# Split-precision feed-forward products with the high weights times both token halves in one matmul, and normed tokens from the fifth pair on in the second feed-forward

## The reference, cut to what matters

```python
D_MODEL = 1024; SEQ = 256; D_FF = 2816

def rmsnorm(x, g):
    return x * rsqrt(mean(x * x, axis=-1) + EPS) * g
def modulate(h, shift, scale):
    return h * (1 + scale) + shift
def swiglu(h, w_in, w_out):
    gate, up = split(h @ w_in, 2, axis=-1)
    return (silu(gate) * up) @ w_out

# first feed-forward, tokens and context tokens
x   = x   + 0.5 * m[2]  * swiglu(modulate(rmsnorm(x, norm_ffn1), m[0], m[1]), w_ffn1_in, w_ffn1_out)
ctx = ctx + 0.5 * mc[2] * swiglu(modulate(rmsnorm(ctx, norm_ffn1), mc[0], mc[1]), w_ffn1_in, w_ffn1_out)
...   # mixer: x = x + m[5] * (mix @ w_mix_out)
# second feed-forward, tokens alone
x = x + 0.5 * m[8] * swiglu(modulate(rmsnorm(x, norm_ffn2), m[6], m[7]), w_ffn2_in, w_ffn2_out)
x = rmsnorm(x, final_norm)
...   # second block
```

## Time and profile before

| | |
|---|---|
| median of 3 runs | 1560.81 us (1559.29 to 1561.89) |
| span of the profiled execution | 1558.5 us |
| the profiled execution against the median | 2.3 us shorter, which includes what lies around the span |
| PE busy | 1417.4 us, 91% |
| DVE busy | 1083.1 us, 69% |
| ACT busy | 597.4 us, 38% |
| POOL busy | 381.5 us, 24% |
| output slices of f1, second round, split halves, on PE | 367.5 to 408.0 us |
| pairs of f2 on PE (258 columns) | 537.5 to 667.1 us |
| output slices of f2 on PE | 667.1 to 730.4 us |

### The profile page before, as it was taken

The page is one execution under the profiler, slowest core; times in us unless marked ns, Lnnn a source line. Parts: engine busy times, 40 slices in busy tenths (PEclk is TensorE's granted clock), DMA queues, the critical chain, the costliest instruction groups (busy, mean ns, idle before and its releaser), DMA issues.

```text
span 1558.5 us, 19836 instructions
## 1 busy us (share of the span) xinstructions
PE 1417.4 (91%) x7349; PEld 1053.8 (68%) x7349; DVE 1083.1 (69%) x2262; ACT 597.4 (38%) x1347; POOL 381.5 (24%) x376
## 2 busy tenths in 40 slices
PE   7899999999999999999999989999987777777777
PEld 5688888889888999999899955665433333233222
DVE  5976775557875687777897476766797666666554
ACT  5222222213556454444566143424343333333222
POOL 0000110001200100001007044545555444444330
PEclk9999999999999999999999999999999999999999
DMA  9754585545642366555545699999999999999997
GB/s 355 265 181 150 169 288 185 164 137 171 213 145 73 108 191 188 172 176 176 161 145 155 242 371 419 422 421 421 421 421 422 421 421 422 421 422 421 422 421 292
DMA packets 86191, 435.96 MB, mean 280 GB/s; under 512 B 9488, under 2 KB 13584, under 8 KB 53072
## 3 DMA queue, kind: packets, MB, share of 16 engines
q0 software_dynamic: 45024, 298.08, 47.6%
q1 hardware_dynamic: 41072, 136.62, 26.9%
HBM read 433.61 MB, written 1.05 MB: 279 GB/s over the span
## 4 chain that ended last, share of the span: by engine, by line
PE 60%; DMA 21%; DVE 13%; ACT 3%; issue 1%; POOL 0%; SPq 0%; ACTq 0%; DVEq 0%; POOLq 0%
PE ps L627 14%; PE ps L628 14%; PE ps L629 14%; DMA ring<-in_puv,AB 13%; PE ps L1059 10%; DMA HF<-in_puv,AB 7%; PE ps L979 5%; DVE WR L1455 2%; DVE ring L2255 1%; DMA ring<-in_w_ada 1%; ACT WR L1079 1%; PE ps L665 1%; DVE HF L2255 1%; DVE AB L1466 1%; PE ps L998 0%
## 5 line engine op out<-in xcount | busy, mean ns | idle before, releaser
L627 PE MATMUL ps<-HR,WR 128*128 128x512 f32 (+2 forms) x1064 | 344.5, 324 | 7.8 <-DVE WR L1455 6.7
L628 PE MATMUL ps<-HR,WR 128*128 128x512 f32 (+2 forms) x1064 | 340.3, 320 | 0.0
L629 PE MATMUL ps<-HR,WR 128*128 128x512 f32 (+2 forms) x1064 | 340.0, 320 | 0.0
L1455 DVE TENSOR_TENSOR WR<-ring,WR 128x1024 fp32r<-128x1024 f32 (+1 forms) x217 | 253.0, 1173 | 113.9 <-ACT WR L1079 113.8
L1079 ACT CAST WR<-ring 128x1024 fp32r<-128x1024 f32 (+1 forms) x217 | 212.5, 986 | 282.8 <-PE ps L629 282.6
L627 PEld LDWEIGHTS ps<-HR,WR 128*128 128x128 f32 x1064 | 203.3, 191 | 25.0 <-issue 7.2
L628 PEld LDWEIGHTS ps<-HR,WR 128*128 128x128 f32 x1064 | 203.4, 191 | 13.9 <-issue 0.2
L629 PEld LDWEIGHTS ps<-HR,WR 128*128 128x128 f32 x1064 | 203.2, 191 | 13.9
L1059 PE MATMUL ps<-AF,AB 128*128 128x512 f32 x264 | 128.3, 610 | 31.5 <-ACT AB L1440 31.5
L1430 ACT ACTIVATE AB<-AB 128x2 f32<-128x2 f32 x129 | 26.2, 203 | 324.6 <-DVE AB L2255 324.6
L627 PE MATMUL ps<-AR,WR 128*128 128x256 f32 (+1 forms) x471 | 147.8, 314 | 2.4 <-DVE AF L1848 2.4
(11 more groups left out here) (339 smaller groups left out, 2345.7 us busy)
## 6 DMA issues: line engine op xcount, KB each, us to landing
AB<-in_w_adaT POOLq DMA_DIRECT2D x56, 512.0 KB, 4.7
ring<-in_f1i SPq DMA_DIRECT2D x44, 512.0 KB, 4.7
ring<-in_f2i SPq DMA_DIRECT2D x44, 512.0 KB, 3.6
ring<-in_w SPq DMA_DIRECT2D x29, 512.0 KB, 3.7
ring<-in_f1o SPq DMA_DIRECT2D x21, 512.0 KB, 3.9
ring<-in_f2o SPq DMA_DIRECT2D x16, 512.0 KB, 4.1
ring<-in_w_ada SPq DMA_DIRECT2D x12, 512.0 KB, 9.4
ring<-in_mi SPq DMA_DIRECT2D x12, 512.0 KB, 4.3
```

Source lines behind the costliest of these rows:

```text
L627: e.matmul(o, l[0], r[0], start=first, stop=False)
L628: e.matmul(o, l[0], r[1], start=False, stop=False)
L629: return e.matmul(o, l[1], r[0], start=False, stop=last)
L1455: e.tensor_tensor(WS[:, m % NSP, 1, 0:nk * cols], ring[:, ring_of(m) % NS, 0:nk * cols], WS[:, m % NSP, 0, 0:nk * cols].bitcast(F32), ALU. ...
```

## The change

`two` stands beside `three`: one matmul with the high weights and a moving operand of high and low tokens side by side (2 x 256 columns), whose results go to the two halves of a PSUM bank, and one with the low weights and the high tokens, 256 columns, added to the first half. `project_apart` walks over the tiles with it. It is used for every product with 256 output columns in the two feed-forwards: the split halves of f1's last round, the eight output slices of f2, and the gates and ups of f2 from pair 4 on (RAWS = 4; the fifth pair). For those pairs the tokens are normed and modulated (in Hs, 256 columns without shift columns): POOL multiplies x by the gain and then by the norm factor (`ft`), ACT adds the shift and rounds, DVE makes the low part; ACT and DVE do this for k = 0 to 2 behind pair 1 and for k = 3 to 7 behind pair 2. The unnormed tokens of pairs 0 to 3 move to AR. Since a result now lies in two halves, they must be added: for pairs 4 to 21 ACT copies the second half of each result to SBUF and DVE adds the first; for output slices DVE makes two additions into XT instead of one, the second waiting for the first.

```diff
+RAWS = 4
+SCALED = {1: range(0, 3), 2: range(3, 8)}
...
-        raw = [Hs[:, n, :, 0:258] for n in range(2)]
+        raw = [AR[:, o:o + 2064].rearrange("p (k c) -> p k c", k=8) for o in (8960, 6656)]
+        ft = AB[:, 0:2048].rearrange("p (k t) -> p k t", k=8)
...
+            def two(o, l, r, first, last):
+                n = r[0].shape[1]
+                apart = o[:, 0:2 * n].rearrange("p (h t) -> p h t", h=2)
+                if first:
+                    e.matmul(apart, l[0], r[2], start=True, stop=False)
+                x = e.matmul(o[:, 0:n], l[1], r[0], start=False, stop=False)
+                return x if first else e.matmul(apart, l[0], r[2], start=False, stop=last)
...
+                            elif j >= RAWS:
+                                project_apart((st_, w, j), H256w, lambda k: dv.at("f2", "h", k))
...
+                        if z - a == 256:
+                            project_apart((st_, "out", rn, d, a), [(Ar[:, 0, k, a:z], Ar[:, 1, k, a:z], Ar[:, :, k, a:z])
+                                                                   for k in range(len(js))], lambda k: dv.at(st_, "act", js[k]))
```

On ACT:

```diff
+                            if j >= RAWS:
+                                q.wait_ge(*dv.at("f2", "act", j - 4))
+                                for w, dst in (("gate", raw_gate(j)), ("up", raw_up(j))):
+                                    q.wait_ge(*mm.at(st_, w, j))
+                                    e.copy(dst, bank_of(st_, w, j)[:, 256:512]).then_inc(*ac.to("low part", w, j))
...
+                            for k in SCALED.get(j, ()):
+                                q.wait_ge(*po.at("f2", "f", k))
+                                e.activation(H256[k][0], ft[:, k, :], ACT.Identity, bias=M[:, 48 + k, 0:1]).then_inc(
+                                    *ac.to("f2", "hi", k))
```

On DVE:

```diff
+                            if j >= RAWS:
+                                q.wait_ge(*ac.at("low part", "gate", j))
+                                e.tensor_tensor(g_, g_, og[:, 0:256], ALU.add).then_inc(*dv.to("ps", st_, "gate", j))
+                                dv.also("shift", "gate", j)
+                                q.wait_ge(*ac.at("low part", "up", j))
+                                e.tensor_tensor(u_, u_, ou[:, 0:256], ALU.add).then_inc(*dv.to("ps", st_, "up", j))
+                                q.wait_ge(*dv.now())
+                                q.wait_ge(*ac.at("silu", j))
+                                e.tensor_tensor(g_, u_, g_, ALU.mult).then_inc(*dv.to("gated", j))
...
+                            for k in SCALED.get(j, ()):
+                                q.wait_ge(*ac.at("f2", "hi", k))
+                                e.scalar_tensor_tensor(out=H256[k][1], in0=ft[:, k, :], scalar=M[:, 48 + k, 0:1],
+                                                       in1=H256[k][0].bitcast(F32), op0=ALU.add, op1=ALU.subtract).then_inc(
+                                                           *dv.to("f2", "h", k))
...
+                            if z - a == 256:
+                                e.scalar_tensor_tensor(out=XT[:, d, o], in0=src[:, 256:512], scalar=m2h[:, d, s:s + 1],
+                                                       in1=XT[:, d, o], op0=ALU.mult, op1=ALU.add).then_inc(
+                                                           *dv.to("low part", st_, d, a))
+                                q.wait_ge(*dv.now())
+                                src = src[:, 0:256]
```

On POOL, behind the sums of squares of the mixer's output ("mo"):

```diff
+            for k in range(8):
+                q.wait_ge(*dv.at("mo", "x", k))
+                e.tensor_scalar(ft[:, k, :], XT[:, k, 0:256], co[:, k, 0:1], None, ALU.mult).then_inc(*po.to("f2", "c", k))
+            for k in range(8):
+                q.wait_ge(*ac.at("root", "mo"))
+                q.wait_ge(*po.at("f2", "c", k))
+                e.tensor_tensor(ft[:, k, :], ft[:, k, :], R(2, 3), ALU.mult).then_inc(*po.to("f2", "f", k))
```

More of the change, by code:

```diff
@@ L388, in program @@
         H512 = [Hp(k, 0, 512) for k in range(8)]
+        H256w = [(*Hp(k, 0, 256), Hs[:, :, k, 0:256]) for k in range(8)]
         qN = AA[:, 0:1024].rearrange("p (i c) -> p i c", i=2)
@@ L1608, in ffn @@
                             og, ou = bank_of(st_, "gate", j), bank_of(st_, "up", j)
+                            if j >= RAWS:
[8 more added lines that the diff above has]
+                                q.wait_ge(*dv.now())
+                                parts((Ar[:, 0, i, :], Ar[:, 1, i, :]), g_, st_, "act", j)
+                                continue
                             q.wait_ge(*mm.at(st_, "gate", j))
```

32 lines of the change are left out of this document (26 added, 6 removed).

## The result

The changed kernel takes 1564.43 us (median of 14 runs, 1560.14 to 1566.28), the kernel before 1560.69 us in the same series (14 runs). The ratio is 1.0019, 95% interval 1.0012 to 1.0026: some 3 us slower (3.7 between the two medians), where 1.1 us faster was forecast. The profiled execution has a span of 1563.1 us, before 1558.5.

The account below looks back on a forecast made before the run. PE's pace was taken to bound mid-f2, DVE's chain the end of f1, DVE nearly full at f2's start. -4.75 - 2.34 + 3.0 + 2.9 + 0.1 = -1.1 us gave 1559.7 us; 8-in-10 range 1554.5 to 1565.0, own range 1557.7 to 1563.9.

Parts of the forecast that it names:

- End of f1: End of f1: DVE's second addition per split half makes q 1 start 3.0 us later, not 1.46 us earlier; bounds 1.5 to 4.0.
- hangs on q 1 and moves with it: Behind q 1: context norm's sum, reciprocal, root and scaling shift by the same 3.0 us as q 1.
- PE's pace: Wide plus narrow matmul replace three narrow ones per block: saves 4.75 us in f2's pairs, 2.34 in its slices.
- 0.2267 + 0.1200 = 0.3467: Cost in us of one block: a wide matmul at the pace of f1's 512-column ones plus a narrow 256-column one.
- The price of two pieces: Other bound for the wide matmul: a moving operand in two pieces costs two narrow matmuls, 0.2399 us.
- Start of f2: First pairs of f2: token low parts (3.2 us) and POOL's hold on DVE (2.0) stall PE 2.9 us; bounds 0.9 and 4.8.
- a single stall: Sign expected in the next profile: PE stalls only once at f2's start, in tiles 7 to 9.
- The 2.3 us by which the low parts were counted early: Start of f2: tile 9's low part, ready at 562.9 us, counted 2.3 us ahead of PE's need, as slack.
- End of f2: Behind f2's last slice: the second addition delays DVE's squares 0.52 us, mostly hidden; 0.1 us taken, at most 0.5.
- collide in full: Rival at f2's start: all sixteen POOL instructions cost DVE 0.48 us each, stall 8.6 us, 1565.4 us; chance 0.13.
- the wide matmul is not two narrow ones: Rival on PE's pace: wide matmul streams as two narrow ones, saving 0.9 us in all, 1565.9 us; chance 0.07.
- what POOL cost was not covered: Rival: POOL works in DVE's waits, f2 stalls 0.5 to 0.9 us, f1 loses 1.5 to 2; 1556.2 us, chance 0.29.

Follow-up runs that it names:

- experiment 6: Kernel before, with the new form (two matmuls a block, two additions) only in the five token halves of f1's last round: 1561.65 us, ratio 1.0007.
- experiment 7: Kernel before, with the new form only in the five context halves of f1's last round: 1564.12 us against 1560.34, ratio 1.0023.
- Experiment 5: Changed kernel plus two plain matmuls of 512 columns, results unused, just ahead of q 1 where PE stood idle: 1561.01 us, ratio 1.0007 to the kernel before.
- experiment 12: As experiment 9, but each weight tile's narrow matmuls all first, then its wide ones: 1556.12 us, ratio 0.9975 to the kernel before.
- experiment 3: As experiment 2, with high and low parts of each token block side by side in memory, one moving piece: ratio 0.9992, f2 183.82 us.
- experiment 8: Kernel before plus only POOL's sixteen instructions of the change, results unused: 1561.74 us, ratio 1.0014, f2 1.63 us longer.
- experiment 9: As experiment 3, with normed tokens used from pair seven instead of pair five: 1555.10 us against 1559.97 for the kernel before, ratio 0.9972.
- experiment 10: As experiment 3, with normed tokens used only from pair nine on: ratio 0.9979 to the kernel before, f2 182.60 us.
- experiment 11: As experiment 10, with the eight token scalings moved from POOL to ACT: 1556.93 us against 1560.34 for the kernel before, ratio 0.9976.
- experiment 2: Changed kernel with the new form only in f2, f1's split halves back to three matmuls and one addition: 1558.42 us, ratio 0.9993 to the kernel before.

## Why the prediction was wrong, and where it was right

- **End of f1: right, but a term is missing.** The forecast had token halves 3.99 us apart (3.98 measured), q 1's low part 3.0 us late (3.1), q 1 at 415.0 (415.47 less 0.40). Its terms make 0.9 us for the token halves (392.4 - 391.5) and 0.52 + 1.56 = 2.1 for the context halves; experiments 6 and 7 measured 0.81 and 2.21. The step that failed is the sentence that what follows "hangs on q 1 and moves with it". It moved with it and another 1.56 us: behind a wait of 2.26 us the clock was at half, a term that the sum does not have. Experiment 5 takes this back (1.6 us). The profile of before held the warning, since it shows such falls elsewhere (below); I looked at the clock of the stretches as they were, and not at what a longer wait would make of it.
- **PE's pace: mis-sized.** 3.7 us in the pairs and 1.35 in the slices instead of 4.75 and 2.34: 2.0 us of gain less, the largest part of the miss. The term that failed is 0.2267 + 0.1200 = 0.3467, which prices the wide matmul at f1's: a block takes 0.350 and 0.352 us. Why, stays open (experiment 12). The price of two pieces, which I kept as a bound, is not the reason (experiment 3). The Trainium skill (TensorE: Matmul & The Clock Gate, Back-to-back issue gap) gives N / 2.4 + 2.5 ns as the gap of an isolated matmul; an estimate from it is 2.5 ns in a slice's block and 5 in a pair's. Measured are 7.6 (0.3599 - 0.3523) and 13.0 (0.3632 - 0.3502), between its rule and my 13.3 and 16.5.
- **Start of f2: nearly right in size, in part for another reason.** 3.4 us against 2.9. The token parts cost what was said (3.3 us of DVE). POOL takes 2.6 us from DVE and not 2.0. But it is not "a single stall" in tiles 7 to 9: POOL's share makes one of its own ahead of tile 5, at 560 us. The 2.3 us by which the low parts were counted early hold for tile 9; tile 5's was 0.1 us early. Experiments 8 and 9 take the two causes apart.
- **End of f2:** from the slices' end to the product's next tile +0.3 us (738.41 - 733.67 against 734.83 - 730.41), 0.1 forecast.
- **Sum by these steps:** f1 +3.1, clock +1.56, pairs -3.7 + 3.4, slices -1.35, end +0.3: +3.3 us. Of the 4.4 us between this and the forecast of -1.1, 2.0 are pace, 1.56 the clock, 0.5 the stall, 0.2 the end, 0.1 f1's chain. The span's +4.6 holds 0.4 ahead of 225 us and 1.0 behind 738 us besides, which no step explains; the ratio's interval, 1.9 to 4.1 us, holds the sum. Either of the two large terms alone turns the sign of the forecast (-1.1 + 2.0, -1.1 + 1.56). The measured 1564.43 us lie inside the stated 1554.5 to 1565.0, near the upper end, and outside the forecast's own range up to 1563.9. Whether the clock fell ahead of q 1 in all 14 executions, and not only in the profiled one, no record shows.
- **Rivals.** None came true. POOL and DVE did not collide in full (2.6 us of 7.7), the wide matmul is not two narrow ones, and what POOL cost was not covered.

Experiments 9 to 12 all beat both kernels, at 0.9972 to 0.9979 of before. Their intervals overlap, so the whole time does not rank them; by the stage experiment 11 is the fastest (181.62 us), then 12 (181.76). All leave f1 alone and let the normed tokens start later.

## What to carry to other kernels

An engine that stands at 19.6 of 20.7 us busy ahead of a wait of PE sets the time there: a form that saves PE matmuls and gives that engine one more instruction per result loses, however good it is elsewhere (apply it per stage, by who waits for whom). When a change lengthens a wait of PE, price what comes behind it at the lower clock too. When work is given to POOL because POOL is idle, count what its instructions with two tensor inputs take from DVE, and put them where the parts that DVE makes for PE are early.

## What the runs showed of the hardware that I had not expected

- The clock falls or not in one and the same place, with the same instructions. The window from 438 to 441 us, right behind a wait of 1.47 us, in the kernel before and in experiment 2, whose instructions are the same up to there but for the addresses:

```profile
438.00:441.00 3.00, 3.00 (x17) 3.00 (x16) 2.64 (x7) 0.83 (x3) 0.00 (x0) 0.52 0.49 162
```

```profile
438.00:441.00 3.00, 3.00 (x27) 3.00 (x26) 2.64 (x8) 0.84 (x3) 0.00 (x0) 1.00 0.55 171
```

  In six of the twelve experiments it stayed full at this place of the program; where it fell, the stretch behind it took 1.5 us more (11.98 us, from 437.26 to 449.24 in the kernel before, against 10.49, from 436.95 to 447.44 in experiment 2). In the profiled executions of the kernel before and of the changed kernel it fell alike, so the two can be compared. But single spans can stand 1.5 us apart by this alone, and a change of 3 us must be read from stages, or from many runs.
- POOL's instructions stretch not only DVE's of two operands from SBUF. A cast with one takes 0.72 us in place of 0.29, while L1666 and L1670, which read PSUM and SBUF, keep their 0.42. The Trainium skill (SBUF — State Buffer, SBUF: two separate sides) says that a GpSimd instruction that reads SBUF and a VectorE instruction with two SBUF inputs, or a GpSimd instruction and a VectorE one in a mode that uses both ports, exclude each other for a whole instruction. Beside L2372 the instructions that are hit agree with it, and the size does not: POOL's stand 1.02 us apart (8.18 / 8), and all but one of DVE's lose 0.26 to 0.53. Beside L2368, which reads SBUF too, the low weight part at 553.94 starts 0.40 us behind one of POOL's and takes 1.23 us, as before.
